# Moving one of four channel groups of a gated linear recurrence from the attention stage to the value products ahead of it

## The chip, the cores and the metric

One Trainium2 chip, one core of it. The metric is the device time of one execution in microseconds. The kernel before takes 4551.89 us, the median of three runs (4550.5 to 4552.7). Matrix products are made of `float32r` operands, split into a high and a low part and multiplied three times.

## What is computed

Two blocks follow one another on 1024 tokens of width 1024. The first is an RWKV-7 branch and a retention branch, merged by gates. The second, which the change touches, is this (cut):

```python
proj = h @ w_in[l]
q, k, v, xr, gr = jnp.split(proj, [...], axis=-1)
attn = diff_attention(q, k, v, lam)            # causal, 4 heads, each the difference of two softmaxes
xc = causal_dwconv(xr, conv_rnn_w[l], conv_rnn_b[l])
y = rg_lru(xc, w_gate_a[l], b_gate_a[l], w_gate_x[l], b_gate_x[l], lru_lambda[l])
y = rms_norm_2(y * jax.nn.gelu(gr), rnn_norm_w[l])
x = x + jnp.concatenate([attn, y], axis=-1) @ w_out[l]
```

`rg_lru` is a linear recurrence over the 1024 tokens, one for each of 512 channels. Its decay and its input gate are sigmoids of small products of `xc` with block diagonal weights, and the input is scaled by a square root of one minus the decay squared. The 512 channels are four groups of 128, one group to a tile of 128 partitions by 1024 tokens. The groups don't depend on each other, nor on the attention.

## The kernel before

The kernel is one program with an order written out by hand for each engine. Each stage is a block of its own: the engines meet at its end, and the next block starts when the last engine is done. Two blocks matter here.

**`mix` (from L2292).** Its last part makes the attention's values: 16 products `j` = 32 to 47 (`for c in range(2)`, in the TensorE part), each of 24 matmuls of 256 columns. ScalarE copies each product out of PSUM (L2530), and six PSUM banks go round, so product `j` needs the copy of product `j-6`. Beside these products the groups `k` = 0 and 1 of the recurrence are worked off. For one group:

- TensorE: `gates(k, 0)` and `gates(k, 1)`, each two fp32 products of 512 columns (L2653, four records) into the PSUM banks 6 and 7. The second waits for `th_a`, which says that ScalarE has read the first.
- ScalarE: `open_a` (L2493, L2494) and `open_x` (L2502, L2503), each two tanh over half a tile; `bend` (L2509), `decay` (L2514) and `decay2` (L2517) over the whole tile; `rise` (L2520 to L2523), a square root between two loads of an activation table.
- VectorE: four steps of convolution `tap` (L2729, L2732), then `admit` (L2737), `spare` (L2742), `enter` (L2747), `run` (the scan, L2752) and `leave` (L2757). The taps of groups 2 and 3 stand there too, behind `leave(0)` and `leave(1)`; they fill the two buffers `xc` that the first groups have left.

ScalarE's part is hung between the copies by the number `j`: `open_a(0)` at 33, `open_x(0)` to `decay2(0)` at 35, `open_a(1)` and `rise(0)` at 37, `open_x(1)` and `bend(1)` at 39, `decay(1)` and `decay2(1)` at 40, `rise(1)` at 41. TensorE has `gates` behind products 32, 34, 36 and 38.

**`attend` (from L2877).** It goes through 32 units: four heads by eight blocks of 128 query rows. A unit `n` of block `t` has a width of `(t+1)*128` keys. Head 0 takes its blocks from 0 to 7, head 1 from 7 to 0, and so on in turn, so that units 7, 8, 23 and 24 are the widest and 15, 16 and 31 the narrowest. One unit is a loop through three engines: TensorE makes the scores (`sc`, L2950 and the mask L2953) into the PSUM banks 0 to 3, VectorE takes the minimum of each row for the two softmaxes (`peak`, L3178), ScalarE takes the exponentials (`exp`, L3036), and TensorE may only then overwrite the banks with the scores of unit `n+1`. Behind that, VectorE forms the difference (`soft`, L3185 to L3189), TensorE turns it (`tr`, L2961), ScalarE copies it out (L3044), TensorE multiplies with the values (`av`, L2970). TensorE's order is `sc(n)`, gates if any, `tr(n-1)`, `av(n-2)`.

The groups 2 and 3 of the recurrence are worked off in between (`NR = 2`, `q` = 0 and 1). For `q` = 1: `gates` behind `sc(12)` and `sc(13)` (L2979), `open_a` at unit 12, `open_x` at 13, `bend` at 14 and `admit` at 14, `decay2` at 20 and `spare` at 21, `decay` at 21, `rise` with its two table loads at 22, `enter` at 23, the scan at 24, `leave` at 25. For `q` = 0 the same stands at units 1 to 9. Four and four dummy products (`keep_warm`, L2995) stand at units 17 and 18. SyncE loads the gates' weights at the stage's start and stores the four groups `gr` when they are done.

`out_up`, the third block, starts with the weights' and the inputs' splitting and the output product.

Of the kernel before, what the change touches and what calls it, by code (L numbers as in the profile page):

```python
# [24 lines left out]
T = 1024  # L25
# [2266 lines left out]
def mix(nc, G, ring, oa, orr, w_a, w_r, w_o, gates, xT, w2, w_v2, a1, qk, v, xg, x2, rope, table, mask, mask_dram, rn, w_ga, w_gx):  # L2292
# [5 lines left out]
    with ExitStack() as ctx:  # L2298
# [23 lines left out]
        early_w, late_w = ([ring.buf[:, (ring.base + 2 * RP + l) % NBUF].rearrange("p k c -> p (k c)")[:, f * T:(f + 1) * T] for f in range(2)] for l in (8, 9))  # L2322
        xc = [table[:, 0], table[:, 1]]
        wg = early_w[1].rearrange("p (a k c) -> p a k c", a=2, k=RT)
        ra, ix = [early_w[0], xr[:, 1, 0:T]], [late_w[0], early_w[0]]
        aa, tt = [xr[:, 0, 0:T], late_w[0]], [late_w[1], late_w[1]]
        line, turned, row_ready = G["line"], sem("turned"), sem("row")
        lstep, lam_e, e_ready, l_ready, wg_in, cstep, conv = (sem(n) for n in ("lstep", "lam_e", "e", "l", "wg_in", "cstep", "conv"))
        gate_a, gate_x, th_a, th_x, ex, ex2, tn, u_ready, m_ready, rt, scan, left = (
# [17 lines left out]
        with nc.Block() as block:  # L2347
# [63 lines left out]
            def _(act):  # L2411
# [78 lines left out]

                def open_a(k):
                    act.wait_ge(gate_a, k + 1)
                    A(ra[k][:, 0:HALF], ps[:, 6], ACT.Tanh, scale=0.5, bias=hb[:, 0, k:k + 1])  # L2493
                    A(ra[k][:, HALF:T], ps[:, 7], ACT.Tanh, scale=0.5, bias=hb[:, 0, k:k + 1]).then_inc(th_a, 1)  # L2494

# [13 lines left out]
                    A(tt[k], ra[k], ACT.Tanh, scale=l1[:, k:k + 1], bias=l1[:, k:k + 1]).then_inc(tn, 1)  # L2509

                def decay(k):
                    if k:
                        act.wait_ge(scan, k)
                    A(aa[k], ra[k], ACT.Exp, scale=hb[:, 2, k:k + 1], bias=hb[:, 2, k:k + 1]).then_inc(ex, 1)  # L2514

# [10 lines left out]
                for j in range(32, 48):  # L2526
                    if j == 33:
                        ring.split_hi(act, 2 * RP + 9)
                    act.wait_ge(made, N1 + j + 1)
                    A(v[:, j % 8, (j - 32) // 8 * CH:(j - 32) // 8 * CH + CH], ps[:, (N1 + j) % NB, 0:CH], ACT.Copy,  # L2530
                      scale=tk[:, j % 8:j % 8 + 1]).then_inc(v_taken, 1)
                    if j == 33:
                        open_a(0)
                    if j == 35:
                        open_x(0)
                        bend(0)
                        decay(0)
                        decay2(0)
                    if j == 37:
                        open_a(1)  # L2540
                        rise(0)
                    if j == 39:
                        open_x(1)
                        bend(1)
                    if j == 40:
                        decay(1)
                        decay2(1)
                    if j == 41:
                        rise(1)
                act.wait_ge(bent, 8)  # L2550
                act.wait_ge(v_taken, 16)

            @block.tensor
            def _(pe):
# [87 lines left out]
                def gates(k, x):  # L2642
                    if x:
                        pe.wait_ge(th_a, k + 1)
                    else:
                        pe.wait_ge(conv, k + 1)
                        if k:
                            pe.wait_ge(th_x, k)
                        else:
                            pe.wait_ge(wg_in, 32)  # L2650
                            pe.wait_ge(h_log, KT)
                    for half in range(2):
                        mm = nc.tensor.matmul(ps[:, 6 + half], wg[:, x, k], xc[k][:, half * HALF:(half + 1) * HALF], start=True, stop=True)  # L2653
                    mm.then_inc(gate_x if x else gate_a, 1)
                for c in range(2):
                    hi, lo = ring.split_ready(pe, 0, 0, 2 * RP + 8 + c)
                    for t in range(T // P):
                        j = 32 + 8 * c + t
                        bank_free(N1 + j)
                        rows = slice(t * P, (t + 1) * P)  # L2660
                        for k in range(KT):
                            mm = product3(nc, ps[:, (N1 + j) % NB, 0:CH], (hp(0, k)[:, rows], hp(1, k)[:, rows]), (hi[:, k], lo[:, k]),
                                          k == 0, k == KT - 1, ring.begun if t == 0 and k == 0 else None)
                        mm.then_inc(made, 1)
                        if c == 0 and t % 2 == 0:
                            gates(t // 4, t // 2 % 2)

            @block.vector
            def _(dve):
# [64 lines left out]
                def admit(k):  # L2734
                    dve.wait_ge(th_x, k + 1)
                    dve.wait_ge(conv, k + 1)
                    V.scalar_tensor_tensor(ix[k], ix[k], 1.0, xc[k], ALU.add, ALU.mult).then_inc(u_ready, 1)  # L2737

                def spare(k):
                    dve.wait_ge(tn, k + 1)  # L2740
# [8 lines left out]
                def run(k):  # L2749
                    dve.wait_ge(u_ready, 2 * k + 2)  # L2750
                    dve.wait_ge(ex, k + 1)
                    V.tensor_tensor_scan(xc[k], aa[k], ix[k], 0.0, ALU.mult, ALU.add).then_inc(scan, 1)  # L2752

                def leave(k):
                    dve.wait_ge(scan, k + 1)
                    dve.wait_ge(bent, 8)
                    V.tensor_tensor(gr[:, k], xc[k], gr[:, k], ALU.mult).then_inc(left, 1)  # L2757
                for k in range(1, HK):
                    ring.part_lo(dve, k)
                    lo(0, k)  # L2760
# [95 lines left out]
                for k in range(2):  # L2856
                    admit(k)
                    spare(k)
                    enter(k)
                    run(k)  # L2860
                    leave(k)
                    for j in range(4):
                        tap(k + 2, j)
                dve.wait_ge(h_done, KT)
                dve.wait_ge(taken, N1 + 32)
                dve.wait_ge(conv, RT)
# [10 lines left out]
def attend(nc, G, ring, qk, v, mask, rn, xc, w_a, w_x, gr, cat, w_next):  # L2877


    NR = 2  # L2880
    with nc.cleanup_on_exit(), ExitStack() as ctx:
        sem = lambda m: nc.alloc_semaphore(f"at_{m}")
        sb = lambda n, s, d=F32: ctx.enter_context(nc.sbuf_tensor("at_" + n, s, d))
# [29 lines left out]
        with nc.Block() as block:  # L2913
# [20 lines left out]
            def _(pe):  # L2934
                pe.wait_ge(rounded, 2)

                def sc(n):
# [4 lines left out]
                    if n == 4:  # L2942
                        pe.wait_ge(th_x, 1)
                    if n == 20:
                        pe.wait_ge(th_x, 2)
                        pe.wait_ge(head_out, 2)
                    for b in range(0, w, HALF):
                        for c in range(2):
# [24 lines left out]
                def gates(q, x):  # L2973
                    if x:
                        pe.wait_ge(th_a, q + 1)
                    else:
                        pe.wait_ge(w_in, 32)
                    for half in range(2):
                        mm = nc.tensor.matmul(ps[:, 1 + 2 * half], wg[:, x, q], xc[q % 2][:, half * HALF:(half + 1) * HALF], start=True, stop=True)  # L2979
                    mm.then_inc(gate_x if x else gate_a, 1)  # L2980

                def flip(g):
                    h, t0, t1 = groups[g]
                    pe.wait_ge(scaled, g + 1)
                    if g == 0:
                        pe.wait_ge(th_x, 2)
                    if g == 2:
                        pe.wait_ge(head_out, 4)
                    for t in range(t0, t1):
                        mm = nc.tensor.transpose(flat_at(h, t // 4)[:, t % 4 * P:(t % 4 + 1) * P], raw[:, h % 3, t], K("ident"))  # L2990
                    mm.then_inc(flipped, 1)
# [3 lines left out]
                        nc.tensor.matmul(ps[:, 1, 0:P], G["ones"][:], G["ones"][:], start=True, stop=True)  # L2995
                for n in range(NU):
                    sc(n)
                    if n in (1, 12):
                        gates(n // 12, 0)
                    if n in (2, 13):  # L3000
                        gates(n // 12, 1)
                    if n == 15:
                        flip(0)
# [21 lines left out]
            def _(act):  # L3025
# [89 lines left out]
                for n in range(NU):  # L3115
# [3 lines left out]
                        turn_out(n - 1)  # L3119
                    if n >= 2:  # L3120
                        take(n - 2)
                    if n in (1, 12):
                        open_a(n // 12)
                    if n in (2, 13):
                        open_x(n // 12)
                    if n in (3, 14):
                        bend(n // 12)
                    if n in (4, 20):
                        decay2(n // 20)
                    if n in (5, 21):  # L3130
                        decay(n // 20)
                    if n in (6, 22):
                        nc.scalar.preload_act_table_set("sqrt_and_others")
                        rise(n // 20)
                        nc.scalar.preload_act_table_set("natural_log_exp_and_others")
# [31 lines left out]
            def _(dve):  # L3167
# [49 lines left out]

                def admit(q):
                    dve.wait_ge(th_x, q + 1)
                    V.scalar_tensor_tensor(ix[:], ix[:], 1.0, xc[q % 2], ALU.add, ALU.mult).then_inc(u_ready, 1)  # L3220

                def spare(q):
                    dve.wait_ge(tn, q + 1)
# [8 lines left out]
                def run(q):  # L3232
                    dve.wait_ge(u_ready, 2 * q + 2)
                    dve.wait_ge(ex, q + 1)
                    V.tensor_tensor_scan(xc[q % 2], aa[:], ix[:], 0.0, ALU.mult, ALU.add).then_inc(scan, 1)

                def leave(q):
                    k = RT - NR + q
                    dve.wait_ge(scan, q + 1)
                    V.tensor_tensor(gr[:, k], xc[q % 2], gr[:, k], ALU.mult).then_inc(y_ready, 1)  # L3240
                for n in range(NU):
                    if n >= 1:
                        soft(n - 1)
                    peak(n, 0)
                    peak(n, 1)
                    if n in (3, 14):
                        admit(n // 12)
                    if n in (5, 21):
                        spare(n // 20)
                    if n in (7, 23):  # L3250
                        enter(n // 20)
                    if n in (8, 24):
                        run(n // 20)
                    if n in (9, 25):
                        leave(n // 20)
                    if n == 10:
                        mean(0)
# [537 lines left out]
```

## Time and profile before

| | us |
|---|---|
| median of three runs | 4551.89 |
| the profiled execution | 4550.82 |
| its span, first to last instruction | 4548.8 |
| value products in `mix` | 3444.4 to 3497.0 |
| `attend`, first score product to last copy | 3498.5 to 3646.6 |

Times in the trace are counted from the span's start. "Busy" of TensorE includes the pipelined tail of each matmul, so matmuls overlap in the records: those of 256 columns start 0.12 us apart and are shown with 0.28 us. The granted clock (PEclk) is TensorE's, as a share of 2.4 GHz; 0.50 is 1.2 GHz. The share of busy time over the whole span tells little of a stage, so the two stages are read by timeline.

### The profile page before, as it was taken

What the parts mean: (1) busy time and instruction counts of PE and PEld (TensorE: products, weight loads), DVE (VectorE), ACT (ScalarE), POOL (GpSimd) and SP (SyncE); (2) the same over time, 40 slices, a digit from 0 to 9 for tenths busy, and PEclk for the clock granted to TensorE, in tenths of its full rate; (3) what the DMA queues carried; (4) which work ended last, traced back from release to release, by engine and by line L of the source; (5) the groups of instructions that cost most, each with busy time, mean ns of one, the idle gap of its engine ahead of it and who ended that gap; (6) DMA issues with size and microseconds to landing.
All of it is one profiled execution on the core that took longest, in us unless ns stands there. A gap on an engine that the chain in (4) does not pass through costs nothing. (4 is left out here: it accounts for less than half of the span.)

```text
span 4548.8 us, 66427 instructions
## 1 busy us (share of the span) xinstructions
PE 4451.2 (98%) x27584; PEld 3640.1 (80%) x27584; DVE 2680.4 (59%) x3924; ACT 1683.3 (37%) x2883; POOL 472.3 (10%) x378
## 2 busy tenths in 40 slices
PE   7999999999999999999999999999999899999999
PEld 5888877778999999999999644788777668888887
DVE  4345544555637776777677776646455855555543
ACT  3234444444424454445444443311224731111111
POOL 0000000000002322333234300000010000000000
PEclk9999999999999999999999999999999999999999
DMA  5343434434430101110112344433120031121222
GB/s 195 116 136 138 149 134 141 146 134 152 165 130 15 46 25 65 60 47 25 65 60 81 101 151 164 144 102 135 52 78 27 19 120 65 70 74 70 104 94 90
DMA packets 156267, 442.05 MB, mean 97 GB/s; under 512 B 17201, under 2 KB 47409, under 8 KB 140865
## 3 DMA queue, kind: packets, MB, share of 16 engines
q1 hardware_dynamic: 140768, 383.72, 24.3%
q0 software_dynamic: 9440, 33.10, 2.0%
q10 hardware_dynamic: 5760, 20.97, 1.3%
q8 instruction: 221, 3.62, 0.3%
q14 instruction: 78, 0.63, 0.0%
HBM read 295.12 MB, written 141.56 MB: 96 GB/s over the span
## 5 line engine op out<-in xcount | busy, mean ns | idle before, releaser
L203 PE MATMUL pr_ps<-uhl,w_split 128*128 128x512 f32 (+1 forms) x1520 | 586.3, 386 | 5.1 <-PEq L266 5.1
L207 PE MATMUL pr_ps<-uhl,w_split 128*128 128x512 f32 (+1 forms) x1520 | 571.2, 376 | 0.0
L206 PE MATMUL pr_ps<-uhl,w_split 128*128 128x512 f32 (+1 forms) x1520 | 570.4, 375 | 0.0
L1590 DVE TENSOR_TENSOR b_G<-b_ps,cst 128x512 fp32r<-128x512 f32 x560 | 381.6, 687 | 65.0 <-PE b_ps L1371 61.6
L138 ACT ACTIVATE w_split<-share 128x2048 fp32r<-128x2048 f32 x64 | 122.6, 1915 | 706.3 <-DVE ou_vc L3611 272.5
L203 PEld LDWEIGHTS pr_ps<-uhl,w_split 128*128 128x128 f32 x1520 | 286.7, 189 | 83.1 <-issue 27.9
L206 PEld LDWEIGHTS pr_ps<-uhl,w_split 128*128 128x128 f32 x1520 | 287.0, 189 | 56.3 <-issue 5.8
L207 PEld LDWEIGHTS pr_ps<-uhl,w_split 128*128 128x128 f32 x1520 | 286.7, 189 | 52.9
L1136 POOL TENSOR_SCALAR b_Mr<-xg 128x512 fp32r<-128x512 f32 x80 | 117.8, 1489 | 1868.2 <-DVE xg L1574 1868.2
L203 PE MATMUL ou_ps<-ou_a,w_split 128*128 128x512 f32 x704 | 276.9, 393 | 7.1 <-DVE ou_a L2248 7.1
L786 DVE COPY pr_stage<-pr_ps 128x256 f32<-128x256 f32 (+1 forms) x92 | 49.7, 540 | 392.2 <-PE pr_ps L207 392.1
L206 PE MATMUL ou_ps<-ou_a,w_split 128*128 128x512 f32 x704 | 275.1, 391 | 0.0
L207 PE MATMUL ou_ps<-ou_a,w_split 128*128 128x512 f32 x704 | 275.0, 391 | 0.0
L1226 ACT ACTIVATE b_EY<-b_ps 128x512 fp32r<-128x512 f32 x320 | 192.4, 601 | 183.1 <-PE b_ps L1385 183.1
L203 PE MATMUL mx_ps<-mx_a,w_split 128*128 128x512 f32 x624 | 251.4, 403 | 0.0
L207 PE MATMUL mx_ps<-mx_a,w_split 128*128 128x512 f32 x624 | 247.0, 396 | 0.0
L206 PE MATMUL mx_ps<-mx_a,w_split 128*128 128x512 f32 x624 | 247.0, 396 | 0.0
L1371 PE MATMUL b_ps<-b_G,b_EY 128*128 128x128 f32 x1600 | 244.5, 274 | 0.0
L1371 PEld LDWEIGHTS b_ps<-b_G,b_EY 128*128 128x128 f32 x1600 | 222.3, 190 | 12.6 <-issue 12.0
L203 PE MATMUL ou_ps<-ou_ext,w_split 128*128 128x512 f32 x576 | 224.1, 389 | 0.0
L206 PE MATMUL ou_ps<-ou_ext,w_split 128*128 128x512 f32 x576 | 224.1, 389 | 0.0
L207 PE MATMUL ou_ps<-ou_ext,w_split 128*128 128x512 f32 x576 | 224.1, 389 | 0.0
(556 smaller groups left out, 9969.9 us busy)
## 6 DMA issues: line engine op xcount, KB each, us to landing
w_ring<-in_w_in SPq DMA_DIRECT2D x40, 1024.0 KB, 5.3
proj<-pr_stage SPq DMA_DIRECT2D x160, 256.0 KB, 2.0
share<-in_w_up SPq DMA_DIRECT2D x24, 1024.0 KB, 4.8
ar<-share SPq DMA_DIRECT2D x32, 512.0 KB, 2.9
b_AR<-ar SPq DMA_DIRECT2D x64, 256.0 KB, 2.9
pr_raw<-proj SPq DMA_DIRECT2D x48, 256.5 KB, 3.5
ff<-ou_vc ACTq DMA_DIRECT2D x24, 512.0 KB, 2.6
share<-ff SPq DMA_DIRECT2D x24, 512.0 KB, 3.7
```

The lines of the kernel that those rows point to most:

```text
L138: self.nc.scalar.activation(self.hl[:, n % NBUF, 0], raw, ACT.Copy).then_inc(self.hi_done, 1)
L203: mm = nc.tensor.matmul(dst, a[0], b[0], start=start, stop=False)
L206: nc.tensor.matmul(dst, a[0], b[1], start=False, stop=False)
L207: return nc.tensor.matmul(dst, a[1], b[0], start=False, stop=stop)
L786: V.tensor_copy(dst, src).then_inc(taken[1], 1)
L1136: F[x]["pool"].done(ts(Mr[x][:], tri[x][e][:], 1.0, None, ALU.mult), f"{n}.Mr")
L1226: L[x]["act"].done(A(EY[x][:, 0:2], both(x)[:, 0:2], ACT.Copy), f"{n}.low{m}")
L1371: mm = mmul(bank(x, 0)[:, q * P:(q + 1) * P], E[x][:, q] if m else Mr[x][:, q], Gs[x][m % 2][:, q], start=True, stop=True)
L1590: L[x]["dve"].done(V.tensor_tensor(Gs[x][m % 2][:], heads(x, 0 if m else 1), rep(K(f"lev{m}"), 4), ALU.mult), f"{n}.G{m}")
```

## The change

Group 2 moves from `attend` to `mix`, where it stands beside the products 42 to 47; `attend` keeps group 3 alone (`NR = 1`), at the places of `q` = 0. In `mix` the group has no buffers of its own: it takes halves of `xr` whose convolutions are done and the ring buffer parts that groups 0 and 1 used, with two added waits (`scan` and `conv`).

```diff
-        ra, ix = [early_w[0], xr[:, 1, 0:T]], [late_w[0], early_w[0]]
-        aa, tt = [xr[:, 0, 0:T], late_w[0]], [late_w[1], late_w[1]]
+        ra, ix = [early_w[0], xr[:, 1, 0:T], xr[:, 0, 0:T]], [late_w[0], early_w[0], xr[:, 1, 0:T]]
+        aa, tt = [xr[:, 0, 0:T], late_w[0], xr[:, 2, 0:T]], [late_w[1]] * 3
...
                 def open_a(k):
                     act.wait_ge(gate_a, k + 1)
+                    if k == 2:
+                        act.wait_ge(scan, 1)
...
                 def decay(k):
-                    if k:
+                    if k == 2:
+                        act.wait_ge(conv, 3)
+                    elif k:
                         act.wait_ge(scan, k)
...
                     if j == 41:
                         rise(1)
+                    if j == 42:
+                        open_a(2)
+                    if j == 43:
+                        open_x(2)
+                        bend(2)
+                        decay(2)
+                        decay2(2)
+                    if j == 45:
+                        rise(2)
...
                         if c == 0 and t % 2 == 0:
                             gates(t // 4, t // 2 % 2)
+                        if c == 1 and t in (2, 3):
+                            gates(2, t - 2)
...
                     for j in range(4):
                         tap(k + 2, j)
+                admit(2)
+                spare(2)
+                enter(2)
+                run(2)
+                leave(2)
...
 def attend(nc, G, ring, qk, v, mask, rn, xc, w_a, w_x, gr, cat, w_next):
-    NR = 2
+    NR = 1
...
                     if n == 20:
-                        pe.wait_ge(th_x, 2)
                         pe.wait_ge(head_out, 2)
...
                     if g == 0:
-                        pe.wait_ge(th_x, 2)
+                        pe.wait_ge(th_x, NR)
...
-                    if n in (1, 12):
+                    if n in (1, 12)[:NR]:
                         gates(n // 12, 0)
-                    if n in (2, 13):
+                    if n in (2, 13)[:NR]:
                         gates(n // 12, 1)
```

The same `[:NR]` stands at each of ScalarE's and VectorE's places of the recurrence in `attend`. `xc[k]` becomes `xc[k % 2]` in `mix` and `xc[q % 2]` becomes `xc[(RT - NR + q) % 2]` in `attend`. The weights' buffer and its two loads shrink from two groups to one.

## Rows read from the trace of the kernel before

**Rows 1.** The page, part 1: TensorE's busy time and share of the span
```profile
PE 4451.2 (98%) x27584; PEld 3640.1 (80%) x27584; DVE 2680.4 (59%) x3924; ACT 1683.3 (37%) x2883; POOL 472.3 (10%) x378
```

**Rows 2.** Waits in attend: who waited for whom, us, times, longest
```profile
ACT at_p L3036 <- DVE at_nb L3178: 35.0, 26, 2.6
```

**Rows 3.** Timeline of TensorE, value products: start, us, engine, line, tile, count
```profile
3469.50 1.88 PE L2653 MATMUL mx_ps<-cst,share 128*128 128x512 f32 x4
```

**Rows 4.** Timeline of ScalarE, end of the value products
```profile
3474.63 0.68 ACT L2502 ACTIVATE share<-mx_ps,rn 128x512 f32<-128x512 f32 x1
...
3475.78 1.25 ACT L2509 ACTIVATE share<-xg,rn 128x1024 f32<-128x1024 f32 x1
...
3482.81 1.06 ACT L2522 ACTIVATE share<-share 128x1024 f32<-128x1024 f32 x1 [1.07 <-DVE share L2742]
3483.89 1.28 ACT L2523 ACT_TABLE_LOAD   x1
3485.19 0.94 ACT L2530 ACTIVATE share<-mx_ps,mx_tk 128x256 f32<-128x256 f32 x2
...
3497.04 0.47 ACT L2530 ACTIVATE share<-mx_ps,mx_tk 128x256 f32<-128x256 f32 x1 [2.37 <-PE mx_ps L207]
```

**Rows 5.** Timeline of VectorE, end of the value products, start of attend
```profile
3483.91 1.23 DVE L2747 TENSOR_TENSOR share<-share 128x1024 f32<-128x1024 f32 x1 [1.13 <-ACT share L2522]
3485.17 2.29 DVE L2752 TENSOR_TENSOR_SCAN cst<-share 128x1024 f32<-128x1024 f32 x1
3487.49 1.22 DVE L2757 TENSOR_TENSOR xg<-cst,xg 128x1024 f32<-128x1024 f32 x1
...
3489.60 3.93 DVE L2732 SCALAR_TENSOR_TENSOR cst<-xg,par,cst 128x1024 f32<-128x1024 f32 x3
3498.04 0.23 DVE L3170 CAST at_id_r<-cst 128x128 fp32r<-128x128 f32 x1 [4.52 <-PEq L2347]
```

**Rows 6.** Timeline of TensorE, attend, units 12 to 14
```profile
3560.64 0.92 PE L2950 MATMUL at_ps<-qk 64*128 64x384 f32 x4
...
3562.23 1.98 PE L2979 MATMUL at_ps<-cst,at_wg 128*128 128x512 f32 x4 [0.31 <-ACT at_ra L3082]
...
3565.70 0.70 PE L2950 MATMUL at_ps<-qk 64*128 64x256 f32 x4
```

**Rows 7.** Timeline of ScalarE, attend, units 11 to 15
```profile
3553.84 0.80 ACT L3036 ACTIVATE at_p<-at_ps,at_nb 128x640 f32<-128x640 f32 x1 [1.77 <-DVE at_nb L3178]
...
3558.79 0.68 ACT L3036 ACTIVATE at_p<-at_ps,at_nb 128x512 f32<-128x512 f32 x1
...
3563.01 0.57 ACT L3036 ACTIVATE at_p<-at_ps,at_nb 128x384 f32<-128x384 f32 x1
...
3569.73 0.38 ACT L3036 ACTIVATE at_p<-at_ps,at_nb 128x128 f32<-128x128 f32 x1
```

**Rows 8.** Timeline of ScalarE, attend, units 22 to 31
```profile
3597.47 1.28 ACT L3133 ACT_TABLE_LOAD   x1
...
3601.14 1.11 ACT L3036 ACTIVATE at_p<-at_ps,at_nb 128x1024 f32<-128x1024 f32 x1
...
3622.42 0.79 ACT L3036 ACTIVATE at_p<-at_ps,at_nb 128x640 f32<-128x640 f32 x1 [1.58 <-DVE at_nb L3178]
...
3636.38 0.37 ACT L3036 ACTIVATE at_p<-at_ps,at_nb 128x128 f32<-128x128 f32 x1 [0.86 <-DVE at_nb L3178]
```

**Rows 9.** Timeline of VectorE, attend, units 23 to 25
```profile
3598.92 2.36 DVE L3178 TENSOR_REDUCE at_nb<-at_ps 128x1 f32<-128x1024 f32 x2 [0.70 <-PE at_ps L2953]
...
3608.05 2.28 DVE L3235 TENSOR_TENSOR_SCAN cst<-at_aa,at_ix 128x1024 f32<-128x1024 f32 x1
...
3611.88 2.08 DVE L3178 TENSOR_REDUCE at_nb<-at_ps 128x1 f32<-128x896 f32 x2
```

**Rows 10.** Timeline of TensorE, attend, unit 1
```profile
3502.07 3.72 PE L2979 MATMUL at_ps<-cst,at_wg 128*128 128x512 f32 x4
```

**Rows 11.** Window: length, busy of each engine, clock, DMA share, GB/s
```profile
3568.00:3576.00 8.00, 7.13 (x55) 5.63 (x54) 5.77 (x20) 6.56 (x25) 0.56 (x1) 1.00 0.17 68
```

More of the change, by code:

```diff
@@ L2652, in gates @@
                     for half in range(2):
-                        mm = nc.tensor.matmul(ps[:, 6 + half], wg[:, x, k], xc[k][:, half * HALF:(half + 1) * HALF], start=True, stop=True)
+                        mm = nc.tensor.matmul(ps[:, 6 + half], wg[:, x, k], xc[k % 2][:, half * HALF:(half + 1) * HALF], start=True, stop=True)
                     mm.then_inc(gate_x if x else gate_a, 1)
@@ L2736, in admit @@
                     dve.wait_ge(conv, k + 1)
-                    V.scalar_tensor_tensor(ix[k], ix[k], 1.0, xc[k], ALU.add, ALU.mult).then_inc(u_ready, 1)
+                    V.scalar_tensor_tensor(ix[k], ix[k], 1.0, xc[k % 2], ALU.add, ALU.mult).then_inc(u_ready, 1)
                 def spare(k):
@@ L2751, in run @@
                     dve.wait_ge(ex, k + 1)
-                    V.tensor_tensor_scan(xc[k], aa[k], ix[k], 0.0, ALU.mult, ALU.add).then_inc(scan, 1)
+                    V.tensor_tensor_scan(xc[k % 2], aa[k], ix[k], 0.0, ALU.mult, ALU.add).then_inc(scan, 1)
                 def leave(k):
@@ L2756, in leave @@
                     dve.wait_ge(bent, 8)
-                    V.tensor_tensor(gr[:, k], xc[k], gr[:, k], ALU.mult).then_inc(left, 1)
+                    V.tensor_tensor(gr[:, k], xc[k % 2], gr[:, k], ALU.mult).then_inc(left, 1)
                 for k in range(1, HK):
@@ L2978, in gates @@
                     for half in range(2):
-                        mm = nc.tensor.matmul(ps[:, 1 + 2 * half], wg[:, x, q], xc[q % 2][:, half * HALF:(half + 1) * HALF], start=True, stop=True)
+                        mm = nc.tensor.matmul(ps[:, 1 + 2 * half], wg[:, x, q], xc[(RT - NR + q) % 2][:, half * HALF:(half + 1) * HALF], start=True, stop=True)
                     mm.then_inc(gate_x if x else gate_a, 1)
@@ L3121, in _ @@
                         take(n - 2)
-                    if n in (1, 12):
+                    if n in (1, 12)[:NR]:
                         open_a(n // 12)
-                    if n in (2, 13):
+                    if n in (2, 13)[:NR]:
                         open_x(n // 12)
-                    if n in (3, 14):
+                    if n in (3, 14)[:NR]:
                         bend(n // 12)
-                    if n in (4, 20):
+                    if n in (4, 20)[:NR]:
                         decay2(n // 20)
-                    if n in (5, 21):
+                    if n in (5, 21)[:NR]:
                         decay(n // 20)
-                    if n in (6, 22):
+                    if n in (6, 22)[:NR]:
                         nc.scalar.preload_act_table_set("sqrt_and_others")
@@ L3219, in admit @@
                     dve.wait_ge(th_x, q + 1)
-                    V.scalar_tensor_tensor(ix[:], ix[:], 1.0, xc[q % 2], ALU.add, ALU.mult).then_inc(u_ready, 1)
+                    V.scalar_tensor_tensor(ix[:], ix[:], 1.0, xc[(RT - NR + q) % 2], ALU.add, ALU.mult).then_inc(u_ready, 1)
                 def spare(q):
@@ L3234, in run @@
                     dve.wait_ge(ex, q + 1)
-                    V.tensor_tensor_scan(xc[q % 2], aa[:], ix[:], 0.0, ALU.mult, ALU.add).then_inc(scan, 1)
+                    V.tensor_tensor_scan(xc[(RT - NR + q) % 2], aa[:], ix[:], 0.0, ALU.mult, ALU.add).then_inc(scan, 1)
                 def leave(q):
@@ L3239, in leave @@
                     dve.wait_ge(scan, q + 1)
-                    V.tensor_tensor(gr[:, k], xc[q % 2], gr[:, k], ALU.mult).then_inc(y_ready, 1)
+                    V.tensor_tensor(gr[:, k], xc[(RT - NR + q) % 2], gr[:, k], ALU.mult).then_inc(y_ready, 1)
                 for n in range(NU):
@@ L3245, in _ @@
                     peak(n, 1)
-                    if n in (3, 14):
+                    if n in (3, 14)[:NR]:
                         admit(n // 12)
-                    if n in (5, 21):
+                    if n in (5, 21)[:NR]:
                         spare(n // 20)
-                    if n in (7, 23):
+                    if n in (7, 23)[:NR]:
                         enter(n // 20)
-                    if n in (8, 24):
+                    if n in (8, 24)[:NR]:
                         run(n // 20)
-                    if n in (9, 25):
+                    if n in (9, 25)[:NR]:
                         leave(n // 20)
```

## The prediction

> **What bounds the kernel now.** First the page: TensorE is busy for 98% of the span [rows 1], so anything that adds work to it where it is dense lengthens the kernel. The stages differ, though. In the value products the timeline shows products of 24 matmuls 2.85 us apart with no gap but for the four pairs of gate products, so TensorE alone sets the pace there. In `attend` the list of waits shows another picture: ScalarE waits 26 times, 35.0 us in all, for VectorE's row minima [rows 2], TensorE waits for ScalarE's exponentials, and no engine is full. What ends last there is a loop through three engines, once for each unit. An extra piece of work costs time in `attend` only where its engine is late for that loop. So the question is what group 2 costs in a stage where TensorE is full and VectorE and ScalarE are half idle, and what its leaving gives back in a stage where most of it lies in gaps.
>
> **Part 1, what `mix` gains in work.** TensorE: two gate slots. One shows 1.88 us of records [rows 3]; their last tail lies over the next product, so I take 1.75 each, 3.5 in all, and 3.8 as the upper end. Nothing hides that, since the products stand without a gap. Their waits are done in time. `gates(2, 0)` needs group 2's convolution. Counting from the last gate slot, 3469.5 + 1.75 + four products of 2.85 = 3482.65 is where product 42 ends; the convolution was done before the step that VectorE takes up at 3483.9 [rows 5]. `gates(2, 1)` comes one slot and one product later, at 3487.25. It needs ScalarE to have read the first slot's result: `open_a(2)` starts behind the table load of `rise(1)` and the copy of product 42, which is the first of the two that start at 3485.19 [rows 4], and two half tanh take 1.15 (from 3474.63 to the next pass at 3475.78, [rows 4]), so it is done near 3486.8. The margin is 0.4 us.
>
> ScalarE: five passes and `rise`. `open_x(2)` starts when TensorE has left the second slot, 3489.0, and `bend`, `decay` and `decay2` follow at 1.14 us steps, the last ending near 3493.9 (1.25 for a full pass, [rows 4]). The copies of products 44 and 45 wait for that, but a copy has six banks of slack, 17 us, so TensorE doesn't stop. `rise(2)` starts behind the copy of product 45: that product ends at 3489.0 + 2 x 2.85 = 3494.7, the copy at 3495.2, the table load of 1.28 at 3496.5, the square root of 1.06 at 3497.6 [rows 4]. The second table load and the last two copies (done near 3501.0) follow.
>
> VectorE: its last three taps ended at 3489.60 + 3.93 = 3493.5 and it then stood idle for 4.5 us [rows 5]. `admit(2)` and `spare(2)`, taken as two steps of 1.2, fit into that idle time, to 3495.9, before the square root needs them. Then comes what is new on the path: `enter`, the scan and `leave`, one behind the other. For group 1 they took from 3483.91 to 3487.49 + 1.22 = 3488.71, which is 4.8 [rows 5]. From 3497.6 that gives 3502.5.
>
> The two added waits and the shared buffers cost nothing: `scan` 1 and `conv` 3 are passed before 3483.9 [rows 5], `open_x(2)` needs `spare(1)`, and `bend(2)` needs `enter(1)`, done at 3485.14 [rows 5], before ScalarE gets there.
>
> Before, the block ended with the copy of 3497.04 + 0.47 = 3497.5 [rows 4], and `attend` began with a cast at 3498.04 [rows 5]. After, it ends with `leave(2)` at 3502.5. **`mix` grows by 5.0 us**: 3.5 of TensorE's slots, and 1.5 in which TensorE is done and VectorE's chain is not. Bounds: 3.5 if the tail were hidden, 6.5 if ScalarE gets to `rise(2)` one copy later.
>
> **Part 2, what `attend` loses in work.** Group 3 keeps group 2's places in units 1 to 9, so those stay as they are. Gone are the places in units 12 to 14 and 20 to 25.
>
> Units 12 to 14: here TensorE was late for the loop. The scores of unit 13 start at 3560.64 without a wait [rows 6], although the exponentials of unit 12 ended at 3558.79 + 0.68 = 3559.47 [rows 7]. Without the first gate slot they would start about 3559.6, so 1.0 is gained. The scores of unit 14 start at 3565.70 without a wait [rows 6], although the exponentials of unit 13 ended at 3563.01 + 0.57 = 3563.6 [rows 7]. Between them lay the second slot, 1.98 and its wait of 0.31 [rows 6]. That is 1.9 more. `open_a`, `open_x`, `bend` and `admit` lay in the same 6 us and give nothing on top. Sum 2.9. A check from the other side: from unit 11's exponentials to unit 15's it was 3569.73 - 3553.84 = 15.9 in head 1 [rows 7], and for the same widths in head 3, without gates but with other extras, 3636.38 - 3622.42 = 14.0 [rows 8]. So at least 1.9.
>
> Units 20 to 25: `decay2` and `decay` end before the minima do; ScalarE still waits for VectorE after them, so they are worth nothing. `rise` is different: the two minima of unit 23 start at 3598.92, each half of 2.36, so the exponential could start near 3600.15 [rows 9], but it started at 3601.14 behind the two table loads [rows 8]. Gain 1.0. The scan (3608.05, 2.28, [rows 9]) made `soft` and then the minima of unit 25 late, which start without a wait at 3611.88 [rows 9]; the loop alone would have been there about 0.4 sooner. `leave` and `spare` lie in gaps. Sum 1.4.
>
> **`attend` shrinks by 4.3 us**, bounds 3.3 and 5.5. The smaller weight load is no term, since the gate products of unit 1 follow the scores at once.
>
> A page speaks against counting table loads by their records alone. The load takes 1.28 us and the next pass starts within 0.1 us of its end (3597.47 + 1.28 = 3598.75; in the value products 3483.89 + 1.28 = 3485.17, next pass 3485.19, [rows 4, 8]). The Trainium skill, "ScalarE: Activation LUTs", section "What ACT_TABLE_LOAD costs", gives 1.38 us of drain beside each load. This trace doesn't show it; by that rule `mix` would grow by 1.4 more and `attend` shrink by 2.8 more, and the kernel would take about 4551.2.
>
> **The clock.** It is at 1.2 GHz for some us where `attend` begins: the gate slot of unit 1 took 3.72 there [rows 10], against 1.88 at 2.4 GHz [rows 3]. TensorE's pause between the blocks grows by 1.5 us, so the low stretch will lie otherwise over unit 0 to 2, and the same holds for the start of `out_up`. I can't place it, so it is no term but a bound: one gate slot at the other level, 3.72 - 1.88 = 1.8, at each of the two places, either way.
>
> **Sum.** +5.0 - 4.3 = +0.7 us. On the profiled execution, 4550.8, that is 4551.5. That execution lies 1.1 below the median of 4551.89, so I forecast **4552.6**. What a measurement of this kernel can tell from no change is 0.2%, 9.1 us; the forecast is far within.
>
> **The rivals.**
> 1. `attend` gives back more. If all of the work that leaves ScalarE were on the loop (four half tanh 2.3, three full passes 3.6, root and two loads 3.6, the durations from [rows 4]) it would shrink by 9.5, net -4.5: 4547.4. Against it: the waits of [rows 2] show ScalarE mostly early. Chance 0.09.
> 2. The tail of `mix` is longer: `open_a(2)` misses its 0.4 us of margin, TensorE stands for it, and `rise(2)`, `enter`, scan and `leave` slide. One full pass and one half late is 2, ordered behind one more copy 3, so net about +4: 4556. Chance 0.10.
> 3. Slower: the clock falls in head 1 and 2. Units 12 to 18 are narrow, and the two gate slots are the densest TensorE work there; dummy products stand behind them at units 17 and 18. Without the slots the clock may fall at unit 13 and stay at 1.2 GHz till the wide units. TensorE is busy for 7.1 of 8 us there at a granted clock of 1.00 [rows 11]; 16 us of that, at nearly double duration (3.72 against 1.88, [rows 3, 10]), would add 14 if all of it were on the loop, 10 if two thirds are. Net +11: 4563. It decides once the granted clock there reads 0.5 for more than 12 us. Against it: head 3's end, without gates, runs its units as fast or faster [rows 8]. The Trainium skill, "TensorE: Matmul & The Clock Gate", section "What's actually happening", says that throttled is the default and that activity lifts it, which is this mechanism. Chance 0.05.
> 4. The move doesn't do what it says, for example because a shared buffer holds group 2 until the end. Then about a whole group's chain stands behind the last product, over 10 us: 4562. The passed waits above speak against it. Chance 0.01.
>
> The forecast's own case keeps 0.75. Its bounds are 3.5 - 5.5 - 1.8 = -3.8 and 6.5 - 3.3 + 1.8 = +5.0 about the median, with one of the two clock places moved; rivals 1 and 2 lie at its edges. Range 4548.0 to 4557.0. Faster by over 0.2% needs more than rival 1 with the clock's help: 0.02. Slower by over 0.2% is rival 3, rival 4 and a little of rival 2: 0.06. The rest, 0.92, is no change.
>
> **What the changed profile should show.** L2653 with 24 records, the last two slots near 3482.7 and 3487.3, the value products' last matmul near 3500.5. VectorE without its 4.5 us of idle time, its `leave(2)` last in the block, at 3502.5, and the first cast of `attend` near 3503.0. In `attend`, L2979 with 8 records, the stretch from unit 11 to unit 15 near 13 us, no wait of VectorE on L2953 of over 1 us there, and no table load at unit 22. `out_up` begins within 2 us of where it did. I am wrong if TensorE stands still among products 42 to 47, if the granted clock falls inside `attend` after unit 3, or if `attend` shrinks by more than 6 or less than 3.

## The result, and the profile after

The changed kernel takes 4560.12 us (median of 16 runs, 4557.91 to 4561.83) against 4550.9 us of the kernel before in its 16 runs: a ratio of 1.002, 95% interval 1.0013 to 1.0027, so 9.2 us slower. I had forecast 4552.6 and a range of 4548.0 to 4557.0, with 0.92 on no change. The profiled execution has a span of 4559.1 us, 10.3 more than the one before. The forecast stood on the median of three runs, 4551.89; the kernel before takes 4550.9 over 16, so that part of it was 1.0 too high, and what is to be held against the 9.2 is the forecast difference of 0.7.

Three lines of the timeline of TensorE and the end of VectorE's in the value products are the first to look at (start, us, engine, line, tile, count):

```profile
3483.07 1.88 PE L2666 MATMUL mx_ps<-cst,share 128*128 128x512 f32 x4
...
3487.63 1.88 PE L2666 MATMUL mx_ps<-cst,share 128*128 128x512 f32 x4
...
3500.61 0.28 PE L207 MATMUL mx_ps<-w_split,mx_ext 128*128 128x256 f32 x1
```

```profile
3495.03 1.22 DVE L2757 SCALAR_TENSOR_TENSOR share<-xg,share 128x1024 f32<-128x1024 f32 x1
3498.12 1.23 DVE L2762 TENSOR_TENSOR xg<-xg,share 128x1024 f32<-128x1024 f32 x1 [1.87 <-ACT share L2526]
3499.38 2.29 DVE L2767 TENSOR_TENSOR_SCAN cst<-xg 128x1024 f32<-128x1024 f32 x1
3501.71 1.23 DVE L2772 TENSOR_TENSOR xg<-cst,xg 128x1024 f32<-128x1024 f32 x1
3503.26 0.23 DVE L3189 CAST at_id_r<-cst 128x128 fp32r<-128x128 f32 x1 [0.32 <-PEq L2347]
```

The new gate slots stand at 3483.07 and 3487.63 (forecast 3482.7 and 3487.3, the timeline of this execution being 0.5 later before the first of them: the fourth slot is at 3469.96, against 3469.50 in [rows 3]), the last product's end is 3.9 us later than before, and VectorE's chain `enter`, scan, `leave` ends at 3502.94. The first cast of `attend` comes at 3503.26, against 3498.04 [rows 5]: 5.2 us later, forecast 5.0. Without the 0.5 of the start, that is from the fourth slot to the first cast, it is 3503.26 - 3469.96 = 33.3 us against 28.5, so `mix` itself has grown by 4.8. `mix` is as forecast.

In `attend`, the first exponentials of units 11 to 16 in ScalarE's timeline of the changed kernel answer to [rows 7]; the first two lines below are those of units 12 and 16 in the kernel before, the others are of the changed kernel:

```profile
3558.11 0.69 ACT L3036 ACTIVATE at_p<-at_ps,at_nb 128x512 f32<-128x512 f32 x1
...
3571.92 0.37 ACT L3036 ACTIVATE at_p<-at_ps,at_nb 128x128 f32<-128x128 f32 x1
```

```profile
3559.66 0.79 ACT L3055 ACTIVATE at_p<-at_ps,at_nb 128x640 f32<-128x640 f32 x1 [1.77 <-DVE at_nb L3197]
...
3563.93 0.69 ACT L3055 ACTIVATE at_p<-at_ps,at_nb 128x512 f32<-128x512 f32 x1
...
3567.23 0.58 ACT L3055 ACTIVATE at_p<-at_ps,at_nb 128x384 f32<-128x384 f32 x1 [1.09 <-DVE at_nb L3197]
...
3569.97 0.47 ACT L3055 ACTIVATE at_p<-at_ps,at_nb 128x256 f32<-128x256 f32 x1 [0.86 <-DVE at_nb L3197]
...
3572.20 0.37 ACT L3055 ACTIVATE at_p<-at_ps,at_nb 128x128 f32<-128x128 f32 x1 [0.66 <-DVE at_nb L3197]
...
3574.74 0.37 ACT L3055 ACTIVATE at_p<-at_ps,at_nb 128x128 f32<-128x128 f32 x1
```

Units 12 to 15 now take 3574.74 - 3563.93 = 10.8 us; before they took 13.8, from 3558.11 to 3571.92. That is 3.0 less, forecast 2.9. And ScalarE waits for VectorE's minima in units 13 to 15 (1.09, 0.86 and 0.66 us), where before the only such wait was one of 0.26 in unit 13. The end of `attend` is another matter. First the last copy out in the kernel before, whose exponential of unit 31 stands in [rows 8], then the changed kernel:

```profile
3645.87 0.69 ACT L3074 ACTIVATE share<-at_ps,rn 128x512 f32<-128x512 f32 x1 [1.67 <-PE at_ps L2990]
```

```profile
3640.33 0.37 ACT L3055 ACTIVATE at_p<-at_ps,at_nb 128x128 f32<-128x128 f32 x1 [0.86 <-DVE at_nb L3197]
...
3643.15 1.28 ACT L3084 ACT_TABLE_LOAD   x1
3644.45 0.30 ACT L3084 ACTIVATE at_fac<-at_ms,eps 128x4 f32<-128x4 f32 x1
3644.76 1.28 ACT L3086 ACT_TABLE_LOAD   x1
3646.06 0.21 ACT L3086 ACTIVATE at_fac<-at_fac 128x4 f32<-128x4 f32 x1
...
3650.35 1.28 ACT L3084 ACT_TABLE_LOAD   x1
3651.65 0.30 ACT L3084 ACTIVATE at_fac<-at_ms,eps 128x4 f32<-128x4 f32 x1
3651.96 1.28 ACT L3086 ACT_TABLE_LOAD   x1
3653.26 0.21 ACT L3086 ACTIVATE at_fac<-at_fac 128x4 f32<-128x4 f32 x1
3655.59 0.69 ACT L3093 ACTIVATE share<-at_ps,rn 128x512 f32<-128x512 f32 x1 [2.13 <-PE at_ps L3009]
```

`norm` makes, for a group of finished blocks, one over the root of a mean square, as an `Ln` followed by an `Exp`; it is called five times, `norm(0)` in unit 11 to `norm(4)`. Ahead of each `Ln` (L3084) and each `Exp` (L3086) of `norm(1)` to `norm(4)` stands an `ACT_TABLE_LOAD` of 1.28 us. The kernel before had none there. The groups of ScalarE in `attend` count them; first the kernel before, then the changed one (line, us and mean ns of one):

```profile
L3133 ACT ACT_TABLE_LOAD x2 | 2.6, 1283 | 0.0
L3135 ACT ACT_TABLE_LOAD x2 | 2.6, 1283 | 0.0
...
L3140 ACT ACT_TABLE_LOAD x1 | 1.3, 1283 | 0.0
```

```profile
L3084 ACT ACT_TABLE_LOAD x4 | 5.1, 1283 | 0.1
L3086 ACT ACT_TABLE_LOAD x4 | 5.1, 1283 | 0.1
...
L2524 ACT ACT_TABLE_LOAD x1 | 1.3, 1283 | 0.0
L2527 ACT ACT_TABLE_LOAD x1 | 1.3, 1283 | 0.0
L3152 ACT ACT_TABLE_LOAD x1 | 1.3, 1283 | 0.0
L3154 ACT ACT_TABLE_LOAD x1 | 1.3, 1283 | 0.0
L3159 ACT ACT_TABLE_LOAD x1 | 1.3, 1283 | 0.0
```

(L2524 and L2527 belong to `mix`, whose last two fall into the same stretch.) 5 loads have become 11. From the exponential of unit 31 to the last copy out it is 3655.59 - 3640.33 = 15.3 us; before it was 3645.87 - 3636.38 = 9.5. Put together, the 10.3 us between the two spans are 5.2 up to the first cast, 4.5 from there to the last copy of `attend`, and 0.6 behind it. So `attend`, which was to shrink by 4.3, has grown by 4.5. The 4.5 are -4.4 in units 12 to 15, 22 and 24, as forecast, +5.8 in the tail, +1.1 in units 27 and 28, +0.5 in unit 23, and +1.5 in places where the clock is another (-0.1 at the start, +0.7 in unit 7, +0.9 in unit 19).

**Why the loads are there.** Behind `norm(0)` in unit 11 the program loads the set `exp_and_others` (L3159 here, L3140 before), for the tanh of the group that came at unit 12. Before, `rise` of that group, in unit 22, ended with a load of `natural_log_exp_and_others`, and so `norm(1)` to `norm(4)` found both functions loaded. With `NR = 1` the group's `rise` is gone and the load behind `norm(0)` has stayed. It leaves the engine with a set that has no logarithm, and in the trace each later `Ln` and `Exp` of `norm` has a load of its own, which no line of kernel.py asks for. The change edits the condition over `rise` and its two loads and leaves the line of unit 11 alone; that line now does what it did not do before.

### The profile page after: what moved, and what is told of

The parts are those of the page before. It is cut to its first block and busy times, and to the rows that moved or that the text cites. A ratio compares the mean times of both kernels' runs of the same rounds, so it can differ in the third digit from the quotient of the medians.

```text
span 4559.1 us, 66441 instructions
## 1 busy us (share of the span) xinstructions
PE 4457.7 (98%) x27584; PEld 3645.5 (80%) x27584; DVE 2679.4 (59%) x3924; ACT 1698.8 (37%) x2895; POOL 473.2 (10%) x378
```

## The experiments

Two theories. **T**: the left-over load and the 8 that follow from it are what the forecast missed. **C**: the falls of TensorE's clock in `attend` are what it missed; the changed profile shows two that the one before hadn't, which was my third rival. All runs of a group were timed beside the kernel before: 4550.56 us in the first four (33 runs), 4550.38 in the last four (33 runs). Each kernel has 11 runs.

**The load taken away.** The changed kernel with one line less:

```diff
                     if n == 11:
                         norm(0)
-                        nc.scalar.preload_act_table_set("exp_and_others")
```

> The changed kernel without the load of the exp_and_others table set behind norm(0) in unit 11 of attend. Theory T (a left-over table switch): in the kernel before, rise of group 3 in unit 22 brought the logarithm's set back; without it the Ln and Exp of norm(1) to norm(4) each load their set, 8 loads. They should be gone here (3 loads in attend instead of 11; 2 if the explicit one alone counts besides rise), the tail from unit 31's exponential to the last copy back from 15.3 to 9.5 us, unit 27 from 5.6 to 4.2, and the kernel near 4552, 8 us below the changed kernel and 1 above the one before. Rival C (the clock's falls at units 7 and 19 and at the tail cost the time): the time stays within 2 us of the changed kernel, 4558 to 4562.

Measured: 4553.05 us (4550.78 to 4554.0), ratio to the kernel before 1.0004 (0.9995 to 1.0012). That is 7.1 us below the changed kernel, and 2.5 above the one before; the interval runs from 2.3 below it to 5.5 above, so this doesn't tell it from no change. In `attend` its groups show the two loads of `rise` and no other, and the tail is 3646.14 - 3636.42 = 9.7 us:

```profile
3636.42 0.37 ACT L3055 ACTIVATE at_p<-at_ps,at_nb 128x128 f32<-128x128 f32 x1 [0.86 <-DVE at_nb L3196]
...
3646.14 0.69 ACT L3093 ACTIVATE share<-at_ps,rn 128x512 f32<-128x512 f32 x1 [1.67 <-PE at_ps L3009]
```

T holds. C does not: the same two falls of the clock are in this profile (below), units 7 and 19 are 6.7 and 5.0 us long, against 6.6 and 4.9 in the changed kernel, and the 7.1 us went all the same.

**The loads alone, nothing moved.** The kernel before, with the set changed that `rise` of the last group loads:

```diff
                         rise(n // 20)
-                        nc.scalar.preload_act_table_set("natural_log_exp_and_others")
+                        nc.scalar.preload_act_table_set("natural_log_exp_and_others" if n < 20 else "exp_and_others")
```

> The kernel before, with one word changed: rise of the last group in unit 22 of attend is followed by a load of exp_and_others in place of natural_log_exp_and_others. No recurrence work moves. Theory T: 8 more table loads (13 in attend), the tail about 5.8 us longer, unit 27 1.4, unit 23 0.5 or more: 7.5 to 9 us slower than before, 4558 to 4560, although nothing was moved. Rival C: the loads lie in gaps of ScalarE and the clock does not fall where it did not; within 2 us of before.

Measured: 4557.18 us (4555.18 to 4558.45), ratio 1.0014 (1.0005 to 1.0023), 6.6 us slower. The groups show 4 and 4 loads at L3065 and L3067 beside the 5 of before, and the tail is 15.2 us:

```profile
3636.50 0.37 ACT L3036 ACTIVATE at_p<-at_ps,at_nb 128x128 f32<-128x128 f32 x1 [0.86 <-DVE at_nb L3178]
...
3639.31 1.28 ACT L3065 ACT_TABLE_LOAD   x1
...
3651.75 0.69 ACT L3074 ACTIVATE share<-at_ps,rn 128x512 f32<-128x512 f32 x1 [2.13 <-PE at_ps L2990]
```

A kernel in which not one operation of the recurrence was moved has most of the slowdown. It is a little under my 7.5. In the profile, unit 27 with its two loads is 5.6 us long, as expected, but unit 28 behind it gives back 0.2; unit 23 costs 0.4 (6.32 us against 5.89), and unit 24 behind it gives all of that back (5.53 against 5.96). With 5.8 in the tail that makes 6.9. The clock falls in unit 7 of this profile too, with nothing moved.

**Where they cost.** The changed kernel with the logarithm's set back from unit 27 on:

```diff
                     if n == 27:
+                        nc.scalar.preload_act_table_set("natural_log_exp_and_others")
                         norm(2)
```

> The changed kernel with the logarithm's set loaded once more ahead of norm(2) in unit 27, so that norm(1) still pays two loads, norm(2) one, norm(3) and norm(4) none. Theory T: 5 loads fewer, the tail back to 9.5 us (5.8 less), unit 27 about 1 us shorter, together 6.5 to 7 us below the changed kernel, near 4553.5. If the loads inside the loop of units were what costs, and not those of the tail, it would be under 3 us. Rival C: no change against the changed kernel.

Measured: 4553.44 us (4551.27 to 4556.77), ratio 1.0005 (0.9997 to 1.0014), 6.7 below the changed kernel, with 5 loads fewer. `norm(1)` still pays two loads in unit 23 (6.35 us long against 5.93 without them), and the time is level with the kernel that has none (4553.05). So what costs is unit 27, net 1.1 us, and above all the tail, where no unit is left to hide behind: four loads, 5.1 us, and the tail of the changed kernel is 5.8 longer. In this profile, an execution of 4556.77 us and the slowest of the 11, the tail is 10.1 us and not the 9.5 that I expected.

**`mix` alone.** The changed `mix`, and `attend` as before with both its groups; group 2 is worked off twice, the second time on other data. The only part that differs from the changed kernel is the whole function:

```diff
 def attend(nc, G, ring, qk, v, mask, rn, xc, w_a, w_x, gr, cat, w_next):
-    NR = 1
+    NR = 2
...
```

> The mix block of the changed kernel with the attend block of the kernel before: group 2 is worked off in both (the second time on data that is no longer its convolution), so this is the cost of the work in mix alone. My prediction's term: 5.0 us above the kernel before, 4556, with the table sets of attend as before (5 loads there). If the clock at the start of attend takes more than its low stretch of before, up to 1.8 more; if the copies or the gate slots stall TensorE, 7 or more.

Measured: 4557.5 us (4556.32 to 4559.3), ratio 1.0014 (1.0005 to 1.0023), so 6.9 us, interval about 2.3 to 10.5. The profile has the first cast at 3503.23, 5.2 us after that of before (4.8 from the fourth gate slot on, as in the changed kernel), to which it adds 0.8 up to the exponential of unit 31 and 1.2 in the tail (10.7 us to the last copy against 9.5), both in stretches in which the granted clock is below 1.00. The term of 5.0 is confirmed by the timeline, and the medians allow it. That the 2 us on top are the clock's is read from this one profile and isn't shown.

**`attend` alone.** `mix` as before, `attend` as changed, without the left-over load. Group 2 is left out:

```diff
 def attend(nc, G, ring, qk, v, mask, rn, xc, w_a, w_x, gr, cat, w_next):
-    NR = 2
+    NR = 1
...
                         norm(0)
-                        nc.scalar.preload_act_table_set("exp_and_others")
```

> The mix block of the kernel before with the attend block of the changed kernel less the left-over load in unit 11. Group 2 of the recurrence is left out altogether, so this is what attend gains by itself. My term: 4.3 us, and 0.4 more for the load that stood before unit 12's exponential: 4546 against 4550.6 for the kernel before. If the clock falls that the changed kernel and the run without the load show at units 7 and 19 come with the lighter attend, they take back up to 1.65: 4547.5. If it is under 2 us, the attend term was wrong too and not just the table loads.

Measured: 4547.77 us (4544.76 to 4549.62), ratio 0.9992 (0.9984 to 1.0001): 2.6 us faster, less than the 4.3 and 0.4 I expected, with an interval that reaches from 7.3 faster to 0.5 slower. Here the profile says more than the medians. From the first exponential to that of unit 31 it is 3629.84 - 3498.78 = 131.1 us against 136.8 before: 5.7 less. By units that is 2.8 in 12 to 15, 1.0 in 22, 0.4 in 24, 0.4 in 11 (the load), and 1.2 at the start, where the clock is low for a shorter time. Without the last it is 4.5, against the 4.7 expected. The tail takes back 0.6 (10.1 us against 9.5). The profiled execution took 4545.34, one of the fastest of the 11, and has none of the falls in the middle of `attend`. The two halves, +6.9 and -2.6, add up to +4.3; together they measure +2.5, and the intervals, each some 8 us wide, hold that difference.

**The tail of `mix` shortened.** On the kernel without the left-over load:

```diff
                         bend(2)
+                        decay2(2)
                         decay(2)
-                        decay2(2)
-                    if j == 45:
+                    if j == 44:
                         rise(2)
...
-                    for j in range(4):
+                    for j in range(2 if k else 4):
                         tap(k + 2, j)
                 admit(2)
                 spare(2)
+                tap(3, 2)
+                tap(3, 3)
                 enter(2)
```

The two decays exchange their buffers, so that the second may be read earlier.

> The changed kernel without the left-over load, and with the tail of mix shortened: decay2 of group 2 ahead of its decay (their two buffers exchanged), rise one product earlier, two of group 3's taps behind spare(2). If the tail behind TensorE's last product is on the path as forecast, enter, scan and leave end 1.2 us sooner, the first cast of attend is about 1.2 us nearer to the last product, and the kernel 1.0 to 1.3 us below the run without the load: 4551.8. If TensorE's two gate slots were all of mix's cost, no difference.

Measured: 4550.21 us (4548.09 to 4553.28), ratio 0.9998 (0.9989 to 1.0007). The last matmul of the value products and the first cast of `attend`, in the timelines of this kernel:

```profile
3498.55 0.28 PE L207 MATMUL mx_ps<-w_split,mx_ext 128*128 128x256 f32 x1
```

```profile
3498.49 1.23 DVE L2774 TENSOR_TENSOR xg<-cst,xg 128x1024 f32<-128x1024 f32 x1
3500.04 0.23 DVE L3192 CAST at_id_r<-cst 128x128 fp32r<-128x128 f32 x1 [0.32 <-PEq L2347]
```

From 3498.55 to 3500.04 it is 1.5 us, where the changed kernel has 3500.61 to 3503.26, 2.65. So 1.2 of the tail was on the path, as forecast. The median is 2.8 below that of the kernel without the load, more than the edit's 1.2; the intervals of both hold such a difference. This profile is also without the low clock at `attend`'s start, and whether that is the rest isn't shown.

**Dummies against the clock's falls.** Again on the kernel without the left-over load:

```diff
                         pe.wait_ge(taken, n - 1)
+                    if n in (5, 17):
+                        for _ in range(8):
+                            nc.tensor.matmul(ps[:, 6 + n % 2, 0:P], G["ones"][:], G["ones"][:], start=True, stop=True)
                     for b in range(t + 1):
```

The profile that this is aimed at has the falls in its windows of 2 us (length, busy time of each engine, granted clock, DMA share, GB/s):

```profile
3538.00:3540.00 2.00, 2.00 (x8) 0.39 (x4) 1.24 (x1) 0.45 (x2) 0.00 (x0) 0.68 0.00 0
3540.00:3542.00 2.00, 2.00 (x11) 1.90 (x10) 1.39 (x2) 0.12 (x1) 0.00 (x0) 0.50 0.00 0
...
3584.00:3586.00 2.00, 2.00 (x12) 1.56 (x9) 0.70 (x1) 0.00 (x0) 0.00 (x0) 0.50 0.00 0
```

> The changed kernel without the left-over load, and with 8 dummy products of TensorE ahead of the value products of unit 5 and of unit 17 (issued in units 7 and 19), where TensorE waits for the exponentials. Rival C, what is left of it: the profile without the load shows the granted clock at 0.5 for 3 to 4 us in unit 7 and in unit 19, which make them 6.7 and 5.0 us long where the kernel before had 5.9 and 4.0. If the falls come from TensorE's pauses there, both units go back and the kernel is up to 1.7 us faster: 4551.4. If they come from something else, the same as without the dummies, 4553, or 0.5 more.

Measured: 4552.57 us (4551.21 to 4555.61), ratio 1.0004 (0.9995 to 1.0013), the same as without the dummies. In the profile no fall is in units 7 and 19; unit 7 is back at 5.9 us, but unit 19 is still 4.6, since there the dummies stand in the way of the next scores, which start 2.13 us after the unit's first exponential (3583.85 - 3581.72) and 1.50 without them (3577.06 - 3575.56, in the profile of `attend` alone). That it was the dummies which kept the falls away isn't shown: the profile of `attend` alone has neither fall and that of the shortened tail none in unit 19, both without dummies. With this cure the falls are worth nothing that the runs can tell.

**Both.**

> Both edits of the last two together, the version that is to beat the kernels: without the left-over load, with the shorter tail and the dummies. By the sum of the two effects 2.5 to 3 us below the run without the load, 4550.3, level with the kernel before. If it is still 2 us above it, the move does not pay with any of these repairs.

Measured: 4551.1 us (4549.07 to 4554.05), ratio 1.0 (0.9991 to 1.0009). I expected 4550.3. No gain from the dummies can be seen; the lowest median of these kernels is that of the one with the shorter tail alone, 4550.21, level with the kernel before (4550.38), and the runs don't tell it from this one. No version was found that beats it.

## Why the prediction was wrong

- **`mix` grows by 5.0**: right. 5.2 in the changed profile, of which 0.5 was there before the new gates; of its own it grew by 4.8, 3.4 at TensorE's last product (forecast 3.5) and 1.3 behind it (forecast 1.5). The shortened tail shows that the part behind TensorE is real and that 1.2 of it can be avoided.
- **`open_a(2)` has 0.4 us of margin, and the copies of 44 and 45 have slack**: right, the value products have no stall. Rival 2, a longer tail, is out.
- **Units 12 to 14 give 2.9**: right, 3.0 and 2.8 in two profiles, counted to the end of unit 15, which takes back 0.35. **`rise` 1.0, scan 0.4**: right, 1.0 and 0.4 by units 22 and 24. Rival 1, that more of ScalarE's work was on the loop, is out.
- **"Group 3 keeps group 2's places in units 1 to 9, so those stay as they are. Gone are the places in units 12 to 14 and 20 to 25"**: this is the step that failed. I counted `rise` as a square root and two loads, and costed their leaving at +1.0 for us. I didn't ask which table set the second load left behind, and who lived on it, so the sum's -4.3 had the leaving of that load as a pure gain and its consequence at nothing. In the kernel before, `norm(1)` to `norm(4)` lived on it. The price of their own 8 loads is 7.1 us by the run without the line (the left-over load itself included, 0.4 in unit 11, of which unit 12 gives back 0.2) and 6.6 by the run with nothing moved. It makes most of the +9.2, and the run without the line is at +2.5. The list of loads to expect in the changed profile named "no table load at unit 22", which came true, and nothing on the four `norm` calls. None of the four rivals has this in it. Of the signs of being wrong that the prediction named, two came: `attend` grew by 4.5 where less than 3 of shrinking was to be the sign, and the granted clock fell after unit 3. The first is the loads; the second is not what cost the 7 us.
- **The rule on the loads**: the Trainium skill, "ScalarE: Activation LUTs", section "What ACT_TABLE_LOAD costs", gives 1.38 us of drain beside the 1.28. The changed trace again has the next pass right behind the load (3643.15 + 1.28 = 3644.43, `Ln` at 3644.45), and the tail's four loads make it 5.8 us longer, 1.45 each. By the figures of the Trainium skill the four would have cost 10.6, an estimate of four times 1.28 + 1.38.
- **The clock, +-1.8 at each of two places**: the places were too few. At `attend`'s start it was worth -0.1 in the changed profile, and what it cost, 0.7 and 0.9, lay in units 7 and 19, which the bound didn't have. The low stretch at `attend`'s start, those in units 7, 19 or 23, and that at its end come and go from one profile to the next, between kernels with the same work there. Rival 3 in its own size, a clock at 1.2 GHz for more than 12 us, did not come. Rival 4 is out with the timeline of `mix`: no wait behind the shared buffers.

Without the left-over line the forecast of 4552.6 would have stood: that kernel took 4553.05. That the two are so close is in part luck, since the forecast's base was 1.0 too high: the difference to the kernel before is +2.5 where +0.7 was forecast. In the profiles, from the fourth gate slot to the last copy of `attend`, it is 3646.14 - 3468.53 = 177.6 us against 3645.87 - 3469.50 = 176.4, so +1.2; the same count gives the changed kernel 3655.59 - 3469.96 = 185.6, so +9.3.

## What to carry to other kernels

An activation table load is a change of state as well as a duration. When work that contains a switch is moved or deleted, list every function behind it on ScalarE up to the next switch, and ask which set each finds now; switches written for the work that left go with it. And a cost that is hidden in a loop of units is paid in full in the tail: the pair of loads of one `norm`, 2.6 us of records, cost 0.4 us in unit 23 or nothing (where unit 24 gave it back), 1.1 in units 27 and 28, and 2.9 behind the last unit.

## What the runs showed of the hardware that I had not expected

- Where a set without the logarithm is active, an `Ln` followed by an `Exp` gets two loads of 1.28 us, one before each (3643.15 and 3644.76), although one set that has both exists and, loaded by hand once, serves all of them with none (the kernel before, and the run without the line). Which set the first of the two brings, the trace doesn't show; that a second load follows before the `Exp` suggests that it is one without `Exp`.
- TensorE's clock falls to 1.2 GHz for a few us inside `attend` in one execution and not in another with the same pause ahead. In the changed kernel the scores of unit 8 wait 2.37 us and then run in 2.53 us, while the granted clock falls from 1.00 to 0.50 (0.58 from 3541 to 3542); behind the same wait in the kernel before they took 1.99, at 3534.73 (unit 8) and at 3603.49 (unit 24). The fall in unit 19 has a pause of only 1.09 us ahead, where the kernel before has 1.08 and no fall. One such fall makes its unit 0.7 to 1.4 us longer (unit 7: 6.59 in the changed kernel and 7.28 with the shortened tail, against 5.89).
